# Hybrid encoder step: gelu times gate moves to ScalarE, rows follow the dots by two slots, and a new pace for stages, picks and rows

## The reference

```python
s1, i1 = lax.top_k(s[:, :, 0], PEER_TOPK)          # 16 of 128 keys, two halves, 8 heads
s2, i2 = lax.top_k(s[:, :, 1], PEER_TOPK)
cand = (s1[..., :, None] + s2[..., None, :]).reshape(m, PEER_HEADS, PEER_TOPK * PEER_TOPK)
top, pos = lax.top_k(cand, PEER_TOPK)
e = (jnp.take_along_axis(i1, pos // PEER_TOPK, axis=-1) * PEER_NKEYS
     + jnp.take_along_axis(i2, pos % PEER_TOPK, axis=-1))
gate = jax.nn.softmax(top, axis=-1)
u = jnp.take(u_tab, e, axis=0)                      # 128 rows of 1024 per frame
act = jax.nn.gelu(jnp.einsum('nkd,nd->nk', u, xb), approximate=False) * gate
vv = jnp.take(v_tab, e, axis=0)
out = jnp.einsum('nk,nkd->nd', act, vv)
```

## Time and profile before

| | before |
|---|---|
| median of 3 runs | 2333.38 us (2332.76 to 2339.48) |
| profiled execution | 2330.52 us |
| its span | 2328.7 us |
| PE busy | 2028.5 us (87%) |
| DVE busy | 1454.5 us (62%) |
| ACT busy | 716.9 us (31%) |
| DMA | 724.48 MB, mean 311 GB/s |

### The profile page before, as it was taken

One profiled execution on the slowest core, in us unless ns is written; L12 is line 12 of the kernel. 1 busy time (PEld: TensorE's weight loads), 2 busy tenths in 40 slices (PEclk: granted clock), 3 DMA queues, 4 the chain that ended last, 5 costly groups with the idle time before them and its releaser, 6 DMA issues.

```text
span 2328.7 us, 24483 instructions
## 1 busy us (share of the span) xinstructions
PE 2028.5 (87%) x8278; PEld 1290.2 (55%) x8278; DVE 1454.5 (62%) x3611; ACT 716.9 (31%) x1842; POOL 609.0 (26%) x549
## 2 busy tenths in 40 slices
PE   8999988699998789999977768999999977777776
PEld 7888886556545456677756536565453632233221
DVE  4122552498656587357878746987755576766764
ACT  2421231242312157334551214325222232121221
POOL 0000000133333122222222213334323344434442
PEclk9999979799999899999988889999999999999999
DMA  6344404699999799899975799899998999999997
GB/s 209 124 151 151 144 18 153 236 354 356 371 417 412 276 349 341 286 344 338 324 267 208 275 363 390 312 356 353 389 365 330 384 402 409 390 400 407 415 387 291
DMA packets 131250, 724.48 MB, mean 311 GB/s; under 512 B 17409, under 2 KB 26113, under 8 KB 61249
## 3 DMA queue, kind: packets, MB, share of 16 engines
q0 software_dynamic: 78336, 570.46, 63.4%
q1 hardware_dynamic: 52176, 150.38, 18.1%
q10 hardware_dynamic: 624, 2.23, 0.2%
HBM read 713.99 MB, written 8.50 MB: 310 GB/s over the span
## 4 chain that ended last, share of the span: by engine, by line
PE 56%; DMA 19%; DVE 17%; ACT 4%; issue 3%; POOL 0%; SPq 0%; DVEq 0%; POOLq 0%; ACTq 0%
PE ps L991 19%; DMA arena<-in_uv,arena 15%; PE ps L685 11%; PE ps L939 11%; DVE arena L1823 6%; PE ps L866 4%; PE ps L890 2%; DMA arena<-in_w_out 1%; PE ps L817 1%; DMA arena<-in_w_a 1%; PE ps L807 1%; PE ps L816 1%; ACT arena L1362 1%; DVE arena L1530 1%; DVE arena L1687 1%
## 5 line engine op out<-in xcount | busy, mean ns | idle before, releaser
L991 PE MATMUL ps<-arena 128*128 128x512 f32 (+1 forms) x1928 | 953.8, 633 | 173.3 <-ACT arena L1362 172.6
L1403 POOL DMA_INDIRECT arena<-in_uv,arena x544 | 607.9, 1117 | 1552.0 <-PE ps L991 1208.3
L1823 DVE CUSTOM_DVE_ANT_0 arena<-arena 128x1024 f32<-128x1024 f32 x544 | 661.7, 1222 | 337.3 <-DMA arena<-in_uv,arena 335.8
L991 PEld LDWEIGHTS ps<-arena 128*128 128x128 f32 (+1 forms) x1928 | 352.6, 194 | 620.4 <-issue 347.8
L1376 ACT ACTIVATE gelu_d<-dots 128x2 f32<-128x2 f32 x272 | 55.4, 204 | 988.5 <-DVE dots L1823 988.1
L939 PE MATMUL ps<-arena 128*128 128x294 f32 (+1 forms) x1152 | 294.2, 412 | 12.7 <-DMA arena<-spill_n 12.7
L939 PEld LDWEIGHTS ps<-arena 128*128 128x128 f32 x1152 | 219.7, 191 | 95.5 <-issue 33.9
L685 PE MATMUL ps<-arena 128*128 128x256 f32 x1152 | 251.7, 382 | 3.0 <-DVE arena L1426 3.0
L685 PEld LDWEIGHTS ps<-arena 128*128 128x128 f32 x1152 | 220.3, 191 | 33.8 <-issue 3.5
L1362 ACT ACTIVATE arena<-ident,share 128x128 f32<-128x128 f32 x450 | 155.5, 386 | 0.0
L866 PEld LDWEIGHTS ps<-arena 128*128 128x128 f32 x1024 | 131.6, 199 | 34.2 <-issue 14.5
(11 more groups left out here) (262 smaller groups left out, 1849.6 us busy)
## 6 DMA issues: line engine op xcount, KB each, us to landing
arena<-in_stream SPq DMA_DIRECT2D x144, 512.0 KB, 3.6
arena<-in_w_a SPq DMA_DIRECT2D x32, 512.0 KB, 7.9
arena<-in_w_out SPq DMA_DIRECT2D x32, 512.0 KB, 8.1
arena<-in_w_q SPq DMA_DIRECT2D x32, 512.0 KB, 8.0
arena<-in_uv,arena POOLq DMA_INDIRECT x544, 8.4
spill<-arena SPq DMA_DIRECT2D x48, 80.0 KB, 5.5
arena<-spill SPq DMA_DIRECT2D x2, 1920.0 KB, 14.0
arena<-in_x_t SPq DMA_DIRECT2D x8, 272.0 KB, 4.2
```

Of the source, the lines that this page charges most:

```text
L991: mm = pe.matmul(ps[0:L, half, :], diag[on_pe(k) % NDIAG][:, 0:L], ring[k % SLOTS][:, D + half * 512:D + (half + 1) * 512], start=False, s ...
L1403: pool.indirect_dma_start(out=ring[kk % SLOTS], out_offset=None, in_=a["uv"], in_offset=bass.IndirectOffsetOnAxis(ap=idx[:, kk:kk + 1], ax ...
L1823: ins = dve.tensor_tensor_reduce(ring[s][:, 0:D], ring[s][:, 0:D], n2p if t == NTILE else n2[t % 2], 1.0, 0.0, ALU.mult, ALU.add, dots[k / ...
```

## The change

Three things change, and the line numbers of the kernel after are higher by up to 15.

- The multiply of gelu by gate leaves VectorE (`share_pair` is gone) and becomes two one-column activations on ScalarE, in `diag_pair`, which now follows the gelu of the same pair at once. `VLAG` goes from 3 to 2: TensorE adds row k in slot k + 2.
- Picks 1 to 7 come every 12 slots (`picks_at`), at slots 0, 12, ... 72; from pick 8 on, slot 16(n - 1) as before.
- `PACE` puts tile 1's work in slots 1 to 91, the projections in slots 92 to 163 and tile 2's work in slots 164 to 238. Between slots 92 and 239 three rows of four are VectorE's (before: every second one, from 104 on), save the first 11 of a tile: 102 rows in all, before 62.

```diff
-        VLAG = 3
+        VLAG = 2
...
-            return 104 <= k < 239 and k % P > 10 and k % 2 == 1
+            return 92 <= k < 239 and k % P > 10 and k % 4 != 0
...
+        def picks_at(kk, part):
+
+            for n in range(LAG, NPICK):
+                first = 12 * (n - LAG) if n < H else TOPK * (n - LAG)
+                if kk == first + PICK_AT[part]:
+                    return [n]
+            return []
...
-        PACE = [(1, 104, BD[1], BG), (104, 186, BG, BD[2]), (186, 239, BD[2], BD[3]), (239, 367, BD[3], stages)]
+        PACE = [(1, 92, BD[1], BG), (92, 164, BG, BD[2]), (164, 239, BD[2], BD[3]), (239, 367, BD[3], stages)]
...
+                if u % (TOPK // 2) == 0:
+                    act.wait_ge(gate_ready, 2 * u // TOPK + 1)
+                act.wait_ge(gelu_ready, u + 1)
+                for j in range(2):
+                    ins = act.activation(share[u % 4][:, j:j + 1], gelu_d[u % 4][:, j:j + 1], ACT.Identity,
+                                         scale=gate[:, 2 * u + j:2 * u + j + 1])
+                ins.then_inc(share_ready, 1)
                 act.wait_ge(share_ready, u + 1)
...
-                if kk % 2 and 0 < kk // 2 <= NS // 2:
-                    diag_pair(kk // 2 - 1)
+                    diag_pair(u)
                 flow.to(stage_at(kk))
-                n = kk // TOPK + LAG
-                if n < NPICK and kk % TOPK == PICK_AT[1] + 1:
+                for n in picks_at(kk - 1, 1):
                     pick_gates(n)
...
-            def share_pair(u):
-                if u % (TOPK // 2) == 0:
-                    dve.wait_ge(gate_ready, 2 * u // TOPK + 1)
-                dve.wait_ge(gelu_ready, u + 1)
-                dve.tensor_tensor(share[u % 4][:, :], gelu_d[u % 4][:, :], gate[:, 2 * u:2 * u + 2], ALU.mult
-                                  ).then_inc(share_ready, 1)
...
-                    share_pair(kk // 2 - 1)
...
-                n = kk // TOPK + LAG
-                if n < NPICK and kk % TOPK == PICK_AT[0]:
+                for n in picks_at(kk, 0):
                     made = pick_halves(n)
```

More of the change, by code:

```diff
@@ L1880, in _ @@
                 flow.to(stage_at(kk))
-                n = kk // TOPK + LAG
-                if n < NPICK and kk % TOPK == PICK_AT[0]:
+                for n in picks_at(kk, 0):
                     made = pick_halves(n)
-                if n < NPICK and kk % TOPK == PICK_AT[1]:
+                for n in picks_at(kk, 1):
                     made = pick_top(n, made)
-                if n < NPICK and kk % TOPK == PICK_AT[2]:
+                for n in picks_at(kk, 2):
                     made = pick_experts(n, made)
```

## The result

| | before | after |
|---|---|---|
| median | 2336.28 us (4 runs, 2332.76 to 2339.48) | 2275.92 us (4 runs, 2272.24 to 2279.95) |
| profiled execution's span | 2328.7 us | 2275.7 us |
| PE busy | 2028.5 us | 1964.3 us |
| DVE busy | 1454.5 us | 1475.5 us |
| ACT busy | 716.9 us | 851.8 us |

What follows compares the result with a forecast made beforehand. Bounds: DMA in A and E, TensorE in B and D, no single engine in C (a chain of small steps). Terms -30 - 36 + 49 - 6 - 1 - 3 = -27 us gave 2306 us, range 2285 to 2332.

Steps and rivals of the forecast that it cites:

- C: Slots 186 to 238, delta (first part, +24) and tail (second, +25) of tile 2: more slots cost +49 us (+27 to +64).
- E: Last stretch, from 1850 us, pure gathering: DMA full at 0.99, so only -1 us (-3 to +1).
- D: Slots 239 to 366, read as TensorE's: fewer waits for diagonals save time, -6 us (-12 to +2).
- B: Slots 104 to 185, second-half projections, TensorE's: 20 rows fewer there, -36 us (-25 to -45).
- A: Slots 1 to 103, delta and tail of tile 1: twelve gathers leave, -30 us (-22 to -38).
- the two corrections: In B: gate stage's diagonal waits vanish, -9 us; VectorE becomes the bound in the last 27 stages, +7 us.
- End: After the last dot: two TensorE rows left instead of four, -3 us.
- The multiply on ScalarE: Gelu times gate on ScalarE: at most 0.4 us a pair, 109 us over 272 pairs, hidden in idle time.
- Rival 3: Diagonal waits mostly go in A, C and D, and C's chain absorbs slots: -57 us, 2276; chance 0.11.
- Rival 4: Share multiply still gates; D, E and the end stay as they are: -17 us, 2316; within the forecast's 0.62.
- Rival 1: C's chain is serial and grows +64 us, taking all back: sum +2, 2335; chance 0.17.
- Rival 2: TensorE's clock falls in C, which grows by 101 us: sum +25, slower, 2358; chance 0.10.

## Why the prediction was wrong, step by step

The forecast was faster by 27 us; it came to 53 in the profiled executions and 60 by the medians. Of the 26 us between 27 and 53, C's term has 15.3, E's 10.8 and D's 4.9; B and the time up to slot 0 take 2.9 and 2.2 back. Two steps failed: the limit that was read for E, where the mechanism was wrong, and the size of C's bill.

- **A, -30: right** (-30.2). Alone, the new pace gave 25.0 of it and the earlier diagonals 3.6.
- **B, -36: right** (-33.1). Rows off TensorE paid there, as the gapless timeline had said. The multiply and lag alone changed B by +0.4, though it cut TensorE's waits for diagonals there from 13.2 to 3.4 us, so the waits of the gate stage were not what I gained. In B's last part TensorE is busy 112.9 us of 120 and VectorE 104.8, so that the bound I moved to VectorE, +7, was not seen either; the two corrections nearly cancelled, which was luck.
- **C, +49: mis-sized** (+33.7, inside its ends of +27 and +64). Its first part was taken at +24 and grew by 16.0 (144.4 to 160.4, to the first matmul of the tail), its second at +25 and grew by 17.7. For the first I took the middle between "all on the chain" and "all absorbed"; more was absorbed than that. The earlier diagonals are not the reason: with the pace alone the first part grows by 16.2 us too, and the second by 22.0. The diagonals' 8.1 us in C are worth 1.8 in the first part and 6.3 in the second, where I had given them no term. Why the chain took in so much was not taken apart. For the second I priced ten gathers at the full rate and bounded the absorption by the 6% of DMA share that were idle: the rate went from 372 GB/s to 409, more than the share left room for. That VectorE is loaded in C's first part was named, but the price of its rows was not seen: 22.7 us of C came back when they moved to TensorE.
- **D, -6: sign right, reason wrong** (-10.9; -14.9 with the old pace). I read "TensorE 400.6 of 420" as a bound, and so allowed only the waits of 16.0 us. With TensorE's work cut by 30 us, and 26 us more on VectorE, D did not move, and with one buffer less it grew by 24.8 before and 12.9 after. The ring has a part in it; what else sets D (tail waits, landings of 54.6 us in after) was not taken apart.
- **E, -1: the failed step** (-11.8, outside its ends). "In E DMA is full at 0.99" took a share of busy time for a limit on the rate. The rate rose to 410 GB/s at nearly the same share when each row held its buffer for two dots less, and fell to 347 with one buffer less. E was bound by the round trip of the ring: landing, dot, two more dots, diagonal, row, issue, landing. But the step was wrong by a few per cent of the rate only: with rows let go 4.5 us sooner a round shortened by 0.8, and in after a buffer less costs E 3.3 us where it cost 71.9 before. E of the kernel after is near a limit that the ring does not set: with 7 buffers it still moved 407 GB/s, with 8 it moved 410.
- **End, -3: right** (-2.8).
- **The multiply on ScalarE**: 0.48 us a pair instead of 0.4; doubling it showed 10 us or nothing, and making it late showed that its place costs more than its length.

The forecast's own lower end does not follow from its terms: A, B and D at their better ends with C at +49 sum to -50, which is 2283 and not 2288. Either is above what was measured.

Rival 3 gave 2276, which is what was measured, but by luck, not for its reasons: it had A at -38 and B at -40 (measured -30 and -33) and nothing for E. It was right on C absorbing the slots (+36) and on D (-12). Rival 4, that D, E and the end stay as they are, is out: they lost 10.9, 11.8 and 2.8 us. Rival 1's serial chain is refuted for the change as it is (C +34, not +64), yet the rows on VectorE have a price there (22.7 us). Rival 2's clock did fall (0.85 to 0.79 in C's first part), and with it C still grew by only 34. The version with the rows on TensorE has 0.96 there and is faster. The Trainium skill (TensorE: Matmul & The Clock Gate, "HAM oscillation — how this bites in real kernels") says that after waits between short pieces of work TensorE's clock is throttled again; the traces agree, with 0.79 where it waited and 0.96 where the rows filled the waits. How much of the 22.7 us is the clock and how much VectorE's 67 us of rows was not separated.

## What to carry to other kernels

Where transfers go round a ring of buffers, read how long a buffer is held between landing and release before calling the stretch DMA-bound; one buffer more or less tests it in one run. A small step may move to a slower engine if it is made earlier there, in line with its consumer. Give an engine's rows to where it has room in that stretch: the same rule helped in B, where TensorE was gapless, and cost in C, where VectorE was busy 0.95 of the first part and its rows stood between the chain's steps.

## What the runs showed of the hardware

- The mean busy share of the DMA engines stays near 1 while the rate differs: 0.93 at 347 GB/s, 0.97 at 387, 0.99 at 399, 1.00 at 410, all in E, with the same gathers of 1.05 MB.
- A ScalarE activation of one column takes 287 ns on average, more than the 204 of gelu on two; two in a row end 0.48 us after the first begins (2063.61 above), so they overlap.
- A busy share of 0.96 did not show that TensorE was the bound of D: with one ring buffer less D took 12.9 us longer at the same share, and with 23 rows moved to VectorE it took the same time at 0.89.
